# A two-layer diffusion trunk on one core: the final norm made on token rows, tile by tile, and each tile stored by itself

## The chip, the core and the metric

The kernel runs on one core of a Trainium2 chip. The number that counts is the device time of one execution in microseconds. The kernel before takes 3027.04 us, the median of 3 runs (3024.94 to 3028.75).

## What is computed

The reference is one inference step of a trunk of two layers over 128 prompt tokens and 512 latent tokens of width 1024. Each layer has a modulated RMS norm, three attention branches beside each other with gates and one output projection, a second norm, and a mixture of 16 experts of which each chooses its tokens. What follows the last layer is all that this case touches:

```
def rms_norm(x, g):
    xf = x.astype(jnp.float32)
    y = xf * lax.rsqrt(jnp.mean(xf * xf, axis=-1, keepdims=True) + EPS)
    return y.astype(x.dtype) * g
...
        x = x + gate2 * expert_choice_ffn(h, w_router, w1, w3, w2)   # end of a layer, for xp and for xs
...
    y_prompt = rms_norm(xp, final_norm)      # (1, 128, 1024)
    y_sample = rms_norm(xs, final_norm)      # (1, 512, 1024)
```

All data is fp32. The mean runs over the 1024 channels of a token, `final_norm` is one weight per channel.

## The kernel before

The residual `x` lies transposed: `x[:, k, t]` is a tile of 128 channels (partition) by 640 tokens (free), for k = 0 to 7; the 512 latent tokens are columns 0 to 511, the 128 prompt tokens are columns 512 to 639. In PSUM there are two tiles of 1024 columns (`mm[0]`, `mm[1]`), one of 1024 (`tp`) and two of 512 (`oo[0]`, `oo[1]`); each hands over by a counting semaphore pair (full, empty). The order on every engine is written out by hand; engines meet only at semaphores.

The experts run in 8 pairs. SyncE streams 24 weight chunks of 1 MB per pair through a ring of 6 buffers, ScalarE rounds each half chunk (`w_hi`), VectorE takes the rest (`w_lo`), TensorE multiplies. What a pair has made (`ye_hi`, `ye_lo`, one row per chosen token) is spread over the tokens by a matmul with a one-hot matrix `hot_t`.

The end of a layer, which the change touches, goes thus in the last layer:

- **Spread.** For k = 0 to 7 TensorE makes two matmuls of 512 columns into `oo[k % 2]` (L1612), and VectorE adds the result, times a gate, to `x[:, k, 0:512]` (`spread`, helper line L2164), which frees `oo[k % 2]` for k + 2. ScalarE squares each finished tile (`last_square`, L2137), VectorE adds the odd squares, GpSimd the even ones (L944).
- **Prompt.** The 16-row results of all experts for prompt tokens come back from DRAM (`ye_ptok`, L2134). TensorE makes the combination in 32 recorded matmuls into `tp` (`combine_p`, L1620), VectorE adds it in 8 instructions to the prompt columns, ScalarE squares those (L2139).
- **Sum of squares over channels.** It is a matmul with a matrix of ones (L1629, L1632), so that the sum of a token stands in every partition of its column.
- **rsqrt.** VectorE scales and adds EPS, ScalarE makes Ln and Exp (`first_rstd`, L1666 and L1668), and VectorE makes one Newton step (`refine_rstd`), all on 128 x 640 elements.
- **Scaling.** VectorE writes `h = x * final * rstd` in 8 instructions.
- **Turning.** For each of 5 token tiles TensorE transposes 8 blocks of `h` into `tp` (L1640), and ScalarE copies `tp` to `tok` (L1649), which holds token rows. There is one `tp`, so the tiles go one after another.
- **Stores.** When all five are done, SyncE issues the store of 4 latent tiles (2 MB, L825) and of the prompt tile (0.5 MB, L826).

Of the kernel before, what the change touches and what calls it, by code (L numbers as in the profile page):

```python
# [255 lines left out]

H_TILES, H_AT = [], {}
# [128 lines left out]
def build(nc, a):  # L388
    ctx = ExitStack()
    with ctx:  # L390
# [38 lines left out]
        tmp = [sb(f"tmp{i}", [P, T]) for i in range(3)]  # L429
        rstd = tmp_r = sb("rstd", [P, T])  # L430
        dw_tmp = [rounded(f"dw_tmp{i}", "tmp2", i * HALF * P, [P, HALF, P]) for i in range(2)]
        const = sb("const", [P, CONST_COLS])
# [111 lines left out]
        slot_in = [sem(f"slot{i}_in") for i in range(RING)]  # L544
        chunks_free = sem("chunks_free")
        mm_full = [sem(f"mm{i}_full") for i in range(2)]
        mm_empty = [sem(f"mm{i}_empty") for i in range(2)]
# [156 lines left out]
        def last_square(k):  # L704

            return (tmp[2][:, 0:NLAT], rstd[:, 0:NLAT], tmp[0][:, 0:NLAT], tmp[1][:, 0:NLAT],
                    *(flat[:, i * NLAT:(i + 1) * NLAT] for i in range(4)))[k]

        last_square_p = flat[:, 3 * D:4 * D].rearrange("p (k t) -> p k t", k=KT)

# [18 lines left out]
        def _(sp):  # L729
# [93 lines left out]

            sp.wait_ge(y_ready, 2)
            sp.dma_start(a["y_sample"][0].rearrange("(t p) c -> p t c", p=P), tok[:, 0:LT, :]).then_inc(y_sent, 16)  # L825
            sp.dma_start(a["y_prompt"][0], tok[:, PRT, :]).then_inc(y_sent, 16)  # L826
            sp.wait_ge(y_sent, 32)
            sp.wait_ge(new_sent, DEPTH * NEW_STORES * 16)
# [6 lines left out]
        def _(pool):  # L835
# [6 lines left out]
            for l in range(DEPTH):  # L842
# [98 lines left out]

                for k in (2, 4, 6):
                    pool.wait_ge(last_sq, l * (KT + 1) + k + 1)
                    last = pool.tensor_tensor(last_square(0), last_square(0), last_square(k), ALU.add)  # L944
                    pool.drain()
                pool.sem_inc(last_even, 1)

# [4 lines left out]
        def _(pe):  # L952
# [181 lines left out]
            for l in range(DEPTH):  # L1134
# [468 lines left out]
                if l + 1 < DEPTH:  # L1603
                    pe.wait_ge(small_in, SMALL_LOADS[l + 1] * 16)
                    wait_t_empty(pe, l, TR["cols_next"])
                    pe.transpose(tp[:, 0:NROWS], rows[:, :], ident[0:NROWS, 0:NROWS]).then_inc(t_full, 1)
                for k in range(KT):
                    j = OO["pairs"] + k
                    wait_o_empty(pe, l, j, PAIRS - 1)
                    for y, ready, n in ((ye_hi, ye_hi_ready, 2 * PAIRS * (l + 1)), (ye_lo, ye_done, PAIRS * (l + 1))):  # L1610
                        pe.wait_ge(ready, n)
                        last = pe.matmul(oo[j % 2][:, :], y[:, k * P:(k + 1) * P], hot_t[:, :],  # L1612
                                         start=(y is ye_hi), stop=(y is ye_lo))
                    last.then_inc(o_full[j % 2], 1)

                pe.wait_ge(ye_back, l * 16 + 16)
                wait_t_empty(pe, l, TR["combine_p"])
                for k in range(KT):
                    for g in range(2):
                        last = pe.matmul(tp[:, k * P:(k + 1) * P], ye_ptok[:, g, k * P:(k + 1) * P],  # L1620
                                         hotw_pt[:, g, :], start=(g == 0), stop=(g == 1))
                last.then_inc(t_full, 1)

                j = MM["norm1"]
# [9 lines left out]


            pe.wait_ge(h_ready, DEPTH * 2 * KT + 1)
            for t in range(TT):
                wait_t_empty(pe, DEPTH, t)
                for k in range(KT):
                    last = pe.transpose(tp[:, k * P:(k + 1) * P], h[:, k, t * P:(t + 1) * P], ident)  # L1640
                last.then_inc(t_full, 1)

# [4 lines left out]
        def _(act):  # L1647
# [98 lines left out]
            for l in range(DEPTH):  # L1746
# [384 lines left out]
                for k in range(KT):  # L2131
                    if k == 2:
                        act.wait_ge(ye_stored, 32 * PAIRS * l + (32 * PAIRS + 32))
                        act.dma_start(ye_ptok, a["ye_pr"].rearrange("e s c -> (e s) c")  # L2134
                                      .rearrange("(g p) c -> p g c", p=P)).then_inc(ye_back, 16)
                    wait_o_read(act, l, OO["pairs"] + k, PAIRS - 1)
                    act.activation(last_square(k), x[:, k, 0:NLAT], ACT.Square).then_inc(last_sq, 1)  # L2137
                wait_t_read(act, l, TR["combine_p"])
                act.activation(last_square_p, x[:, :, NLAT:T], ACT.Square).then_inc(last_sq, 1)  # L2139


            load_log()
            first_rstd(DEPTH, 0)
            for t in range(TT):
                wait_t_full(act, DEPTH, t)
                copy(tok[:, t, :], tp[:, :]).then_inc(t_empty, 1)
            act.drain()
            act.sem_inc(y_ready, 2)

# [4 lines left out]
        def _(dve):  # L2154
# [150 lines left out]
            dve.sem_inc(x_ready, 1)  # L2305
            dve.sem_inc(layer_free, 1)

            for l in range(DEPTH):
# [547 lines left out]
                for k in range(KT):  # L2856
                    spread(k, PAIRS - 1)
                    if k in (4, 6):
# [3 lines left out]
                dve.sem_inc(last_odd, 1)  # L2862
                wait_t_full(dve, l, TR["combine_p"])
# [7 lines left out]

            refine_rstd(DEPTH, 0, 0, D)
            for k in range(KT):
                last = stt(h[:, k, :], x[:, k, :], col("final", k), rstd[:, :], ALU.mult, ALU.mult)
            last.then_inc(h_ready, 1)

# [34 lines left out]
```

## Time and profile before

| | us |
|---|---|
| median of 3 runs | 3027.04 |
| the profiled execution, its own time | 3027.11 |
| its span in the profile | 3025.3 |
| TensorE busy in the span | 2827.1 (93%) |
| VectorE busy | 2013.2 (67%) |
| ScalarE busy | 1643.7 (54%) |
| last matmul of the last expert pair begins | 2966.43 |
| store of y_sample issued | 3017.04 |

The profiled execution is 1.8 us longer than its span: that much lies outside what the profile shows. Busy time is a sum over the whole span; the stretch of the change is the last 60 us, and in it no engine is busy for long. There the chain of waits must be read, not the shares. The granted clock of TensorE has two levels, 1.00 (2.4 GHz) and 0.50 (1.2 GHz); a slice with a number between holds a change from one to the other.

### The profile page before, as it was taken

The numbers are of one execution on the slowest core, as the hardware profiler recorded it, in microseconds if no ns is written. First come the engines' busy times: TensorE is split into PE (matmuls) and PEld (weight loads), VectorE is DVE, ScalarE is ACT, GpSimd is POOL, SyncE is SP. The second block draws the span as 40 slices with busy tenths as digits, with TensorE's granted clock in tenths as the row PEclk, the third lists the DMA queues.
The fourth block names the chain that finished last, engine by engine and source line by source line (L and its number), as shares of the span: only waits on it lengthen the run. The fifth ranks groups of instructions, "written<-read, shape, count | busy, mean of one in ns | idle before, by whom it ended". The sixth has DMA issues, their size and how long they took to land.

```text
span 3025.3 us, 45336 instructions
## 1 busy us (share of the span) xinstructions
PE 2827.1 (93%) x16026; PEld 2222.8 (73%) x16026; DVE 2013.2 (67%) x3103; ACT 1643.7 (54%) x2435; POOL 266.0 (9%) x294
## 2 busy tenths in 40 slices
PE   6999999989989999999989999999998999999995
PEld 3868966979947777777658797688896677777774
DVE  3463256473469999999845524655646799999994
ACT  3253344263257777777634524433524677777773
POOL 0050012030010000000002300200201000000000
PEclk9999999999989999999999999999999999999997
DMA  7102200222289999999821021013043799999991
GB/s 296 60 32 78 74 30 29 85 73 98 106 302 354 335 336 336 336 335 337 303 73 63 29 96 57 1 56 128 29 147 139 287 338 333 337 337 337 332 347 54
DMA packets 280123, 564.13 MB, mean 186 GB/s; under 512 B 14040, under 2 KB 19872, under 8 KB 279328
## 3 DMA queue, kind: packets, MB, share of 16 engines
q1 hardware_dynamic: 273056, 543.25, 50.2%
q10 hardware_dynamic: 4448, 9.87, 0.9%
q0 software_dynamic: 2464, 8.91, 0.8%
q8 instruction: 102, 1.67, 0.2%
q14 instruction: 53, 0.43, 0.0%
HBM read 546.36 MB, written 15.63 MB: 186 GB/s over the span
## 4 chain that ended last, share of the span: by engine, by line
PE 65%; DVE 14%; issue 7%; ACT 5%; ACTq 2%; POOL 2%; DVEq 1%; DMA 1%; POOLq 1%; SPq 0%
PE mm L1050 23%; PE mm L1571 20%; DVE w_lo L2156 7%; PE mm L1073 6%; PE mm L1103 2%; PE mm L1295 2%; DVE x L2164 2%; ACTq L2077 2%; POOL scratch L864 2%; ACT scratch L1649 1%; ACT w_hi L1649 1%; PE oo L1007 1%; DVE scratch L2156 1%; PE oo L1317 1%; POOLq L863 1%
## 5 line engine op out<-in xcount | busy, mean ns | idle before, releaser
L2156 DVE TENSOR_TENSOR w_lo<-ring,w_hi 128x1024 fp32r<-128x1024 f32 x768 | 911.9, 1219 | 86.6 <-ACT w_hi L1649 70.0
L1649 ACT ACTIVATE w_hi<-ring 128x1024 fp32r<-128x1024 f32 x768 | 803.4, 1059 | 277.9 <-PE mm L1571 255.4
L1050 PE MATMUL mm<-h_hi,ring_lo 128*128 128x320 f32 (+1 forms) x1344 | 315.1, 316 | 2.5 <-DVE h_lo L2156 2.0
L1050 PEld LDWEIGHTS mm<-h_hi,ring_lo 128*128 128x128 f32 (+1 forms) x1344 | 224.6, 189 | 16.3 <-issue 14.4
L1571 PE MATMUL mm<-w_lo,xa_hi 128*80 128x512 f32 x512 | 204.7, 400 | 18.1 <-DVE w_lo L2156 11.8
L2156 DVE TENSOR_TENSOR ring_lo<-ring,dw_hi 128x512 fp32r<-128x512 f32 (+1 forms) x104 | 70.1, 676 | 207.2 <-ACT dw_hi L1649 206.2
L1571 PE MATMUL mm<-w_lo,xb_hi 128*128 128x512 f32 x512 | 203.9, 398 | 0.0
L1571 PE MATMUL mm<-w_hi,xa_lo 128*80 128x512 f32 x512 | 202.6, 396 | 0.0
L1571 PE MATMUL mm<-w_hi,xa_hi 128*80 128x512 f32 x512 | 201.4, 393 | 0.0
L1571 PE MATMUL mm<-w_hi,xb_hi 128*128 128x512 f32 x512 | 200.0, 391 | 0.0
L1571 PE MATMUL mm<-w_hi,xb_lo 128*128 128x512 f32 x512 | 199.4, 389 | 0.0
L1649 ACT ACTIVATE dw_hi<-ring 128x512 fp32r<-128x512 f32 (+1 forms) x104 | 64.0, 619 | 226.2 <-PE mm L1050 225.3
L1649 ACT ACTIVATE scratch<-mm 16x1024 f32<-16x1024 f32 (+7 forms) x140 | 99.4, 720 | 103.4 <-PE mm L1103 42.0
L1050 PE MATMUL mm<-h_lo,dw_hi 128*128 128x320 f32 (+1 forms) x576 | 132.2, 311 | 0.0
L1050 PE MATMUL mm<-h_hi,dw_hi 128*128 128x320 f32 (+1 forms) x576 | 132.2, 311 | 0.0
L1571 PEld LDWEIGHTS mm<-w_lo,xa_hi 128*80 128x80 f32 x512 | 76.4, 149 | 61.4 <-DVE w_lo L2156 18.3
L923 POOL DMA_INDIRECT merged<-h_rows,stat x16 | 27.8, 1739 | 1041.5 <-DVE w_lo L2156 1001.0
L1050 PE MATMUL mm<-h_lo,dw_tmp 128*128 128x320 f32 x512 | 117.7, 311 | 0.0
L1050 PE MATMUL mm<-h_hi,dw_tmp 128*128 128x320 f32 x512 | 117.7, 311 | 0.0
L1743 ACT ACTIVATE scratch<-mm,stat 128x640 f32<-128x640 f32 (+1 forms) x80 | 56.6, 708 | 102.8 <-DVE stat L2292 102.8
L1571 PE MATMUL mm<-w_lo,hidb_hi 128*128 128x512 f32 x256 | 101.5, 397 | 11.7 <-DVE w_lo L2156 11.7
L1571 PEld LDWEIGHTS mm<-w_hi,xb_hi 128*128 128x128 f32 x512 | 96.1, 188 | 20.9
(325 smaller groups left out, 6071.7 us busy)
## 6 DMA issues: line engine op xcount, KB each, us to landing
ring<-in_w_ff SPq DMA_DIRECT2D x384, 1024.0 KB, 6.4
ring<-in_w_ada SPq DMA_DIRECT2D x48, 1024.0 KB, 7.4
ring<-in_w_gate SPq DMA_DIRECT2D x24, 1024.0 KB, 6.1
ring<-in_w_in SPq DMA_DIRECT2D x16, 1024.0 KB, 9.5
ring<-in_w_o SPq DMA_DIRECT2D x8, 1024.0 KB, 7.9
x_spill<-x SPq DMA_DIRECT2D x2, 2560.0 KB, 12.6
ring<-in_w_br_da SPq DMA_DIRECT2D x4, 1024.0 KB, 6.4
ring<-in_w_br_mla SPq DMA_DIRECT2D x4, 1024.0 KB, 5.2
```

The costliest lines, as they stand in the source:

```text
L863: pool.drain()
L864: pool.tensor_tensor(p1, p1, p2, ALU.add).then_inc(p_mixed, 1)
L1050: last = pe.matmul(out[0:width, lo:hi], w_, h_[:, k, lo:hi], start=(k == 0 and i == 0), stop=(k == KT - 1 and i == 2))
L1073: last = pe.matmul(h_out(j)[:, lo:hi], w_, o_[:, k, lo:hi], start=(k == 0 and i == 0), stop=(k == 3 and i == 2))
L1103: last = pe.matmul(mm[j % 2][:, 0:width], h[:, k, t * P:(t + 1) * P], weight(c, k, c0, c0 + width), start=(k == 0), stop=(k == KT - 1))
L1295: last = pe.matmul(mm[j % 2][:, at:at + hi - lo], ml_q[hd % 2][0:MQ, t * P:(t + 1) * P], ml_k[hd % 2][0:MQ, lo:hi], start=True, stop=True)
L1571: last = pe.matmul(out[0:rows_, bank:bank + 512], a_[:, k, 0:rows_], b_[n % SPLITS][:, kk, :], start=(k == 0 and i == 0), stop=(k == KT - ...
L1649: return act.activation(out, in_, ACT.Copy, scale=scale)
L1743: act.activation(out, mm[j % 2][:, 0:width], ACT.Exp, bias=stat[:, sum_at:sum_at + 1], accum_out=stat[:, sum_at + 16:sum_at + 17])
L2077: act.drain()
L2156: return dve.tensor_tensor(out, in0, in1, op)
L2164: return dve.scalar_tensor_tensor(out=out, in0=in0, scalar=s, in1=in1, op0=op0, op1=op1)
```

## The change

Nothing changes before the last spread of the last layer. From there:

- TensorE turns `x`, not `h`. While it spreads, it transposes block k - 2 of token tiles 0 and 1 into `mm[0]` and `mm[1]`, two transposes ahead of the matmuls of each k from 2 on, and blocks 6 and 7 behind the spread. Tile 2 goes into `oo[0]` and `oo[1]` behind `combine_p`, the prompt tile into `tp` when the prompt columns are done, and tile 3 into `mm[0]` when tile 0 has been read for the last time. The order of the output tiles is 0, 1, 2, prompt, 3.
- ScalarE squares each turned tile from PSUM in two halves of 512 columns with an accumulated sum per token (`accum_out`); Ln and Exp work on 2 columns for tiles 0 and 1, and on 3 columns for the others.
- VectorE adds the two halves, makes mean plus EPS, waits for Exp, makes the Newton step on 2 or 3 columns, and writes `tok = turned * rstd * final_row` straight from PSUM, two instructions of 512 columns per tile. The first mean stands in its order between the last spread and the prompt's additions.
- `final_row`, the weight as a row in all 128 partitions, is loaded by one broadcasting DMA (512 KB written), issued by SyncE behind the last weight chunk.
- SyncE stores each tile when it is ready.
- The squares of `x`, their additions on VectorE and GpSimd, the matmuls with ones, the scaling of `h`, the last transposes and ScalarE's copies are gone in the last layer.

```diff
+Y_ORDER = (0, 1, 2, PRT, LT - 1)
+        final_row = nc.alloc_sbuf_tensor_at("final_row", [P, D], FP32, offset=place["tmp2"])
+        def y_parts(n):
+            at = (mm[0], mm[1], None, tp, mm[0])[n]
+            return [oo[half][:, 0:512] if at is None else at[:, 512 * half:512 * half + 512] for half in range(2)]
...
 SyncE
-            sp.wait_ge(y_ready, 2)
-            sp.dma_start(a["y_sample"][0].rearrange("(t p) c -> p t c", p=P), tok[:, 0:LT, :]).then_inc(y_sent, 16)
-            sp.dma_start(a["y_prompt"][0], tok[:, PRT, :]).then_inc(y_sent, 16)
-            sp.wait_ge(y_sent, 32)
+            sp.wait_ge(lgt_ready, DEPTH)
+            sp.wait_ge(h_ready, DEPTH * 2 * KT)
+            sp.dma_start(final_row[:, :], a["final_norm"].partition_broadcast(P)).then_inc(final_in, 16)
+            for n, t in enumerate(Y_ORDER):
+                sp.wait_ge(y_ready, n + 1)
+                sp.dma_start(a["y_sample"][0][t * P:(t + 1) * P, :] if t < LT else a["y_prompt"][0], tok[:, t, :])\
+                    .then_inc(y_sent, 16)
+            sp.wait_ge(y_sent, 16 * TT)
...
 TensorE
+                def turn_y(out, t, k):
+                    return pe.transpose(out[:, k % 4 * P:(k % 4 + 1) * P] if out is oo[k // 4] else out[:, k * P:(k + 1) * P],
+                                        x[:, k, t * P:(t + 1) * P], ident)
                 for k in range(KT):
                     j = OO["pairs"] + k
                     wait_o_empty(pe, l, j, PAIRS - 1)
+                    if l + 1 == DEPTH and k >= 2:
+                        for t in range(2):
+                            if k == 2:
+                                wait_mm_empty(pe, DEPTH, t)
+                            turn_y(mm[t], t, k - 2)
...
+                if l + 1 == DEPTH:
+                    for k in (6, 7):
+                        wait_o_read(pe, l, OO["pairs"] + k, PAIRS - 1)
+                        for t in range(2):
+                            last = turn_y(mm[t], t, k)
+                            if k == 7:
+                                last.then_inc(y_turned, 1)
... (combine_p)
+                if l + 1 == DEPTH:
+                    for k in range(KT):
+                        last = turn_y(oo[k // 4], 2, k)
+                    last.then_inc(y_turned, 1)
+                    pe.wait_ge(x_ready, 1 + 2 * DEPTH)
+                    for k in range(KT):
+                        last = turn_y(tp, PRT, k)
+                    last.then_inc(y_turned, 1)
+                    pe.wait_ge(y_ready, 1)
+                    for k in range(KT):
+                        last = turn_y(mm[0], LT - 1, k)
+                    last.then_inc(y_turned, 1)
+                    break
...
 ScalarE
             load_log()
-            first_rstd(DEPTH, 0)
-            for t in range(TT):
-                wait_t_full(act, DEPTH, t)
-                copy(tok[:, t, :], tp[:, :]).then_inc(t_empty, 1)
-            act.drain()
-            act.sem_inc(y_ready, 2)
+            for lo, hi in ((0, 2), (2, TT)):
+                for n in range(lo, hi):
+                    act.wait_ge(y_turned, n + 1)
+                    for half, part in enumerate(y_parts(n)):
+                        act.activation(h_flat[:, 512 * (2 * n + half):512 * (2 * n + half + 1)], part, ACT.Square,
+                                       accum_out=stat[:, 2 * n + half:2 * n + half + 1])
+                act.drain()
+                act.sem_inc(y_squared, 1)
+                act.wait_ge(y_mean, 1 if lo == 0 else 2)
+                act.activation(stat[:, 32 + lo:32 + hi], stat[:, 24 + lo:24 + hi], ACT.Ln)
+                act.drain()
+                act.activation(stat[:, 32 + lo:32 + hi], stat[:, 32 + lo:32 + hi], ACT.Exp, scale=-0.5)\
+                    .then_inc(y_root, 1)
...
 VectorE
+            def y_mean_of(lo, hi):
+                dve.wait_ge(y_squared, 1 if lo == 0 else 2)
+                sums = stat[:, 2 * lo:2 * hi].rearrange("p (n h) -> p n h", h=2)
+                tt(stat[:, 24 + lo:24 + hi], sums[:, :, 0], sums[:, :, 1], ALU.add)
+                dve.drain()
+                ts(stat[:, 24 + lo:24 + hi], stat[:, 24 + lo:24 + hi], 1.0 / D, ALU.mult, EPS, ALU.add).then_inc(y_mean, 1)
... (behind spread(7), ahead of the wait for combine_p)
+                    y_mean_of(0, 2)
... (at the end)
+            dve.wait_ge(final_in, 16)
+            for lo, hi in ((0, 2), (2, TT)):
+                if lo:
+                    y_mean_of(lo, hi)
+                v, r_, t_ = stat[:, 24 + lo:24 + hi], stat[:, 32 + lo:32 + hi], stat[:, 40 + lo:40 + hi]
+                dve.wait_ge(y_root, 1 if lo == 0 else 2)
+                tt(t_, r_, r_, ALU.mult)
... (three more small operations, a drain behind each)
+                for n in range(lo, hi):
+                    for half, part in enumerate(y_parts(n)):
+                        at = slice(512 * half, 512 * half + 512)
+                        last = stt(tok[:, Y_ORDER[n], at], part, stat[:, 32 + n:33 + n], final_row[:, at],
+                                   ALU.mult, ALU.mult)
+                    dve.drain()
+                    dve.sem_inc(y_ready, 1)
```

## Rows read from the trace of the kernel before

**Rows 1.** Chain of waits, last 60 us: start us, duration us, engine, tile, line.
```profile
2970.72 3.30 PE oo L1612 x6
...
2977.51 5.17 PE tp L1620 x32
...
2984.93 1.06 ACT merged L2139
...
3001.62 1.98 PE tp L1640 x8
...
3003.63 1.03 ACT merged L1649
...
3015.95 1.02 ACT merged L1649
```

**Rows 2.** Stretches, TensorE: from:to, us, busy (count), granted clock, DMA share, GB/s.
```profile
2967.00:2968.00 1.00, 0.00 (x0) 1.00 0.00 0
...
2970.00:2971.00 1.00, 0.61 (x3) 0.74 0.15 29
...
2980.00:2981.00 1.00, 1.00 (x8) 0.64 0.00 0
2981.00:2982.00 1.00, 1.00 (x11) 1.00 0.00 0
...
2990.00:2992.00 2.00, 0.00 (x0) 0.74 0.00 0
```

**Rows 3.** Timeline of the spread, all engines: start, us, engine, line, operation, out<-in.
```profile
2971.74 0.63 PE L1612 MATMUL oo<-hot_t,ye_hi 128*128 128x512 f32 x1
2972.17 0.63 PE L1612 MATMUL oo<-hot_t,ye_lo 128*128 128x512 f32 x1
...
2974.72 0.68 DVE L2156 TENSOR_TENSOR rstd<-rstd,tmp 128x512 f32<-128x512 f32 x1
...
2977.70 0.75 DVE L2164 SCALAR_TENSOR_TENSOR x<-oo,mod,x 128x512 f32<-128x512 f32 x1
```

**Rows 4.** Timeline of TensorE: eight transposes at clock 1.00.
```profile
2877.45 1.04 PE L1524 MATMUL tp<-const,merged 128*128 128x128 f32 x8
```

**Rows 5.** Timeline of ScalarE: activations with accumulated sum, and table loads.
```profile
636.71 0.68 ACT L1964 ACTIVATE scratch<-mm,stat 128x512 f32<-128x512 f32 x1
...
637.37 0.29 ACT L1966 ACTIVATE stat<-stat,bc 128x1 f32<-128x1 f32 x1
...
229.60 1.28 ACT L1837 ACT_TABLE_LOAD   x1
231.70 0.22 ACT L1837 ACTIVATE scratch<-scratch 128x20 f32<-128x20 f32 x1 [0.82 <-DVE scratch L2161]
231.98 1.28 ACT L1839 ACT_TABLE_LOAD   x1
```

**Rows 6.** Timeline of VectorE: small operations, and larger ones on PSUM.
```profile
234.03 0.18 DVE L2161 TENSOR_SCALAR scratch<-scratch 128x20 f32<-128x20 f32 x1
234.28 0.18 DVE L2156 TENSOR_TENSOR scratch<-scratch 128x20 f32<-128x20 f32 x1
...
2969.91 1.41 DVE L2164 SCALAR_TENSOR_TENSOR x<-oo,mod,x 128x512 f32<-128x512 f32 x2 [0.63 <-PE oo L1612]
...
2982.70 2.16 DVE L2164 SCALAR_TENSOR_TENSOR x<-tp,mod,x 128x128 f32<-128x128 f32 x8 [4.25 <-PE tp L1620]
```

**Rows 7.** DMA issues, whole span: out<-in, queue, count, KB each, median us to landing.
```profile
h_rows<-merged ACTq DMA_DIRECT2D x8, 512.0 KB, 3.6
...
out_y_prompt<-merged SPq DMA_DIRECT2D x1, 512.0 KB, 7.4
...
ctx_in<-in_cache_mla_krope SPq DMA_DIRECT2D x2, 16.0 KB, 3.1
```

**Rows 8.** Timeline of SyncE's queue, last 122 us.
```profile
2903.43 42.79 SPq L819 DMA_DIRECT2D ring<-in_w_ff  x15
3017.04 0.39 SPq L825 DMA_DIRECT2D out_y_sample<-merged  x1
```

More of the change, by code:

```diff
@@ L545, in build @@
         chunks_free = sem("chunks_free")
+        y_turned, y_squared, y_mean, y_root, final_in = (sem("y_turned"), sem("y_squared"), sem("y_mean"), sem("y_root"),
+                                                         sem("final_in"))
         mm_full = [sem(f"mm{i}_full") for i in range(2)]
@@ L707, in last_square @@
                     *(flat[:, i * NLAT:(i + 1) * NLAT] for i in range(4)))[k]
+        def y_parts(n):
+            at = (mm[0], mm[1], None, tp, mm[0])[n]
+            return [oo[half][:, 0:512] if at is None else at[:, 512 * half:512 * half + 512] for half in range(2)]
+        h_flat = h[:, :, :].rearrange("p k t -> p (k t)")
         last_square_p = flat[:, 3 * D:4 * D].rearrange("p (k t) -> p k t", k=KT)
@@ L940, in _ @@
                 pair(PAIRS - 1, True)
-                for k in (2, 4, 6):
+                for k in (2, 4, 6) if l + 1 < DEPTH else ():
                     pool.wait_ge(last_sq, l * (KT + 1) + k + 1)
@@ L945, in _ @@
                     pool.drain()
-                pool.sem_inc(last_even, 1)
+                if l + 1 < DEPTH:
+                    pool.sem_inc(last_even, 1)
         @block.tensor
@@ L1633, in _ @@
                 last.then_inc(mm_full[j % 2], 1)
-            pe.wait_ge(h_ready, DEPTH * 2 * KT + 1)
-            for t in range(TT):
[L1638 to L1641, printed above, removed]
         @block.scalar
@@ L2135, in _ @@
                                       .rearrange("(g p) c -> p g c", p=P)).then_inc(ye_back, 16)
[L2136 to L2139, printed above, removed]
-            load_log()
-            first_rstd(DEPTH, 0)
-            for t in range(TT):
-                wait_t_full(act, DEPTH, t)
-                copy(tok[:, t, :], tp[:, :]).then_inc(t_empty, 1)
-            act.drain()
-            act.sem_inc(y_ready, 2)
+                    if l + 1 < DEPTH:
+                        wait_o_read(act, l, OO["pairs"] + k, PAIRS - 1)
+                        act.activation(last_square(k), x[:, k, 0:NLAT], ACT.Square).then_inc(last_sq, 1)
+                if l + 1 < DEPTH:
+                    wait_t_read(act, l, TR["combine_p"])
+                    act.activation(last_square_p, x[:, :, NLAT:T], ACT.Square).then_inc(last_sq, 1)
+            load_log()
+            for lo, hi in ((0, 2), (2, TT)):
[11 more added lines that the diff above has]
+                    .then_inc(y_root, 1)
         @block.vector
@@ L2857, in _ @@
                     spread(k, PAIRS - 1)
-                    if k in (4, 6):
+                    if k in (4, 6) and l + 1 < DEPTH:
                         dve.wait_ge(last_sq, l * (KT + 1) + k)
@@ L2861, in _ @@
                         dve.drain()
-                dve.sem_inc(last_odd, 1)
+                if l + 1 < DEPTH:
+                    dve.sem_inc(last_odd, 1)
+                else:
+                    y_mean_of(0, 2)
                 wait_t_full(dve, l, TR["combine_p"])
@@ L2869, in _ @@
                     dve.sem_inc(s, 1)
[L2872 to L2875, printed above, removed]
+            dve.wait_ge(final_in, 16)
[6 more added lines that the diff above has]
+                dve.drain()
+                tt(t_, t_, v, ALU.mult)
+                dve.drain()
+                ts(t_, t_, -0.5, ALU.mult, 1.5, ALU.add)
+                dve.drain()
+                tt(r_, r_, t_, ALU.mult)
+                dve.drain()
+                for n in range(lo, hi):
[3 more added lines that the diff above has]
+                                   ALU.mult, ALU.mult)
+                    dve.drain()
+                    dve.sem_inc(y_ready, 1)
         return nc
```

## The prediction

> **What bounds the kernel now.** I read the page first: TensorE is busy 93% of the span, and the chain that ended last lies on it for 65%. None of that bears on this change, which touches only the last 60 us. There I read the chain of waits in order of time. The reader is to see in it that behind the spread (2970.72 to about 2978) one engine works at a time: 32 matmuls for the prompt from 2977.51, which end at 2982.68, one square on ScalarE at 2984.93, and then nothing that the rows show of transposes until 3001.62 [rows 1]. Between lie the ones-matmuls, Ln and Exp, the Newton step and the scaling, one behind the other on 640 columns. From 3001.62 each tile takes eight transposes (1.98) and one copy (1.03), and as there is one PSUM tile for them, these alternate: (3015.95 - 3003.63) / 4 = 3.08 us per tile [rows 1]. Only then, at 3017.04, is a store issued [rows 8]; the span ends at 3025.3, 8.3 us later, with every engine idle. From the end of the prompt's matmuls to the last copy (3016.97) that is 34.3 us, and 42.6 us to the end of the span.
>
> **The spread gets longer.** Two matmuls of a k start 0.43 us apart (2971.74, 2972.17) while the clock is low, which it is from 2970.7 on [rows 2, 3]. Eight transposes take 1.98 at the low clock [rows 1] and 1.04 at the high one [rows 4], so 0.25 and 0.13 each. Before, TensorE is not full in this stretch: per k its work is 0.86, and the chain through VectorE (0.75 for the addition, [rows 3]) gives about 1.04. With two transposes per k the work is 0.86 + 0.50 = 1.36, and TensorE becomes the bound of the spread. Six k's (2 to 7) from 2970.72 make 8.2, to 2978.9; with 0.2 until the last result stands and 0.04 + 0.75 on VectorE the last addition ends at 2979.9, against 2978.45 before: 1.4 later. (The two VectorE additions of squares, 0.68 each [rows 3], go away; they delayed k = 5 and k = 7 by some 0.6, and that gain is in this count, because TensorE is the bound now.) At the high clock the transposes would be hidden and the spread end at 2978 or before: that is the other end, 1.9 better. I take the low clock, since the fall within 2970 to 2971 follows a pause of TensorE around the last expert results (idle from 2967 to 2968 [rows 2]), and that pause stays. The transposes of blocks 6 and 7: two fit in before the last addition ends, two come behind it, 0.5, so that the prompt's matmuls begin at 2980.4 and not at 2977.5.
>
> **The prompt's matmuls** take 5.17 before, of which about 3.3 at the low clock, until it rises at 2980.6, and 1.9 at the high one [rows 1, 2]. I take the same 5.2 and hold C = 2985.6 as their end: 2.9 later than before. If the clock did not rise at all they would take 32 x 0.22 = 7.0.
>
> **Beside them, hidden.** ScalarE squares tiles 0 and 1. The next instruction behind an activation with accumulated sum on 128 x 512 starts 0.66 after it (636.71 to 637.37 [rows 5]), so a half costs 0.66, a tile 1.32, two tiles 2.6: from 2980.4 to 2983.1. VectorE's mean, two small operations of 0.25 each with their drain [rows 6], gives 2983.7; Ln 0.22, a table load 1.28, Exp 0.22 give 2985.5. VectorE waits for these squares in front of the prompt's additions; behind it in its order stand these additions and then the whole output, and their input comes at C = 2985.6, so that wait has 1.9 us of cover and the root 2.3 more. If the squares took 2 us longer, the excess would move everything. The table set with Ln is loaded early, in the idle time of the spread. The squares of x, GpSimd's additions (hidden before too) go away for nothing gained.
>
> **The weight row.** SyncE's last weight chunk is issued at 2946.2 [rows 8]; the broadcast goes out behind it and is wanted at C + 2.2 = 2987.8. No row shows a broadcast of this size. The nearest, 512 KB between SBUF and DRAM, land in 3.6 and 7.4 [rows 7]; priced by the byte from the 16 KB load (3.1, [rows 7]) it would be 99 us. I take under 10, by the rows of its size, and cost it at nothing: 41.6 us cover it.
>
> **Behind C, the path.** (1) Eight additions for the prompt, 2.16 [rows 6], to 2987.8; in this time TensorE turns tile 2 and ScalarE squares it, done by 2988.1 at the high clock, 2989 at the low one. (2) Four small operations of the Newton step at 0.25 with drain: 1.0, to 2988.8. (3) Tile 0: two instructions of 128 x 512 on PSUM with two operands, 0.70 each when back to back [rows 6], with a drain 1.5, to 2990.3. The prompt tile is turned in parallel and squared by 2991.2 at the latest. (4) Tile 3 needs the buffer of tile 0: eight transposes, 1.04 at the high clock and 1.98 at the low one. Before, the clock falls at about 2990.5, some 2.4 us after the last matmul [rows 2]; here only transposes with pauses follow C. I take the low clock, to 2992.3. (5) Its squares 1.32 and a drain, to 2993.75. (6) Now the root for tiles 2, prompt and 3. ScalarE's load for Ln is issued ahead of the wait of its activation: at L1837 the load ran at 229.60 and the activation waited for VectorE behind it [rows 5]. So the load (1.28) covers VectorE's mean (0.5). Ln 0.22, load 1.28, Exp 0.22 follow: 3.1 in all, to 2996.85. (7) Newton step 1.0, to 2997.85. (8) Three tiles at 1.5, to 3002.35. Tiles 0 and 1 leave VectorE before 2992, so their stores are long gone. Sum behind C: 16.75, against 34.3 before.
>
> **The stores.** The last one is 512 KB of the same shape as h_rows from the same buffer, 3.6 from issue to landing [rows 7]. Two others go out 1.5 and 3.0 us before it. The upper bound is the 7.4 of y_prompt, which stood behind 2 MB; the lower one is 3.1, the landing of 16 KB [rows 7]. I take 3.6 and 0.4 for the end behind the landing (3017.48 + 7.4 = 3024.9 against 3025.3): 4.0 against 8.3 before.
>
> ScalarE's table loads are where the Trainium skill gives another answer. The trace has a load at Ln and another at the Exp behind it, 1.28 each [rows 5]. The Trainium skill (ScalarE: Activation LUTs, "Table sets: the hidden batching unit") says that one set holds both functions and that a change from one to the other needs no load; the trace disagrees here. By the page the sum would be two loads less, 2.6.
>
> The Trainium skill speaks against the split stores: DMA: Bandwidth & Descriptors, "Bandwidth", asks for 1 MiB or more per DMA for 75% of the peak. The row of the 512 KB store is the duration that is used here; that its rate falls when three follow each other no row shows.
>
> **Sum.** 2.9 lost up to C; 34.3 - 16.75 = 17.55 won behind it; 4.3 won at the stores: 18.95. Span 3025.3 - 18.95 = 3006.35. The profiled execution is 3027.11, 1.8 above its span, and 0.07 from the median of 3027.04, so the time is 3008.2.
>
> **Rivals.** (a) *The clock stays at 1.2 GHz through the prompt's matmuls*, because they begin behind a spread with short pauses and stop-and-go work. For it: the clock was low for 10 us of nearly full TensorE before [rows 2]. Against: it rose 3.1 us after the dense stretch began. C moves by 1.85: 3010.1. Chance 0.15.
> (b) *The last three stores get in each other's way*: at 7.4 for the last landing, 3.8 more: 3012.0. For it: the row of y_prompt. Against: its 2 MB in front, for which here are at most 1 MB, sent earlier. Chance 0.08.
> (c) *Ln and Exp need no load between them*: 3005.6. Against: rows 5 show one at either. Chance 0.03.
> (d) *The transposes and squares cost less than counted* (the clock high for tile 3, or the spread at its upper end): 0.9 to 2.8 less, 3005.4 to 3007.3. Chance 0.10.
> (e) *Slower than before: the weight row comes late.* All 128 partitions read the same 4 KB of DRAM, and VectorE waits for it in front of all ten output instructions. Every microsecond above 41.6 is paid in full; from 41.6 + 18.85 = 60.4 the kernel is no faster, from 66.5 it is slower by over 0.2%. At 99 us the time is 3008.2 + 57.4 = 3065.6. For it: no row shows such a load. Against: both rows of its size. Chance 0.03.
> (f) *The waits in VectorE's order eat the gain*: if tiles 0 and 1's squares held it 4 us past C (each half at 2 us instead of 0.66), 3012. Chance 0.03.
>
> **From these to the numbers.** The forecast has 0.58, with its own range 3006.5 to 3010. The predicted time is 3008.2. The range 3003.5 to 3013 leaves out (e), the far ends of (b) and (c) together with (d), and what I have not thought of. About 0.2% (6 us) is what a measurement of this kernel can tell from no change. Faster by over 0.2% needs less than 3021: all cases but (e), 0.96; within 0.2%: 0.01; slower: 0.03.
>
> **What would show it right or wrong.** In the changed profile: the last addition of the spread at about 2979.9, C at 2985.6 and a clock that is 1.00 before C; a table load on ScalarE ahead of the wait at Ln and one at each Exp; the root for tiles 0 and 1 ready ahead of the prompt's last addition; a wait of VectorE for ScalarE from about 2991.8 to 2996.85 as the only long one behind C; three pairs of output instructions at the end, and 4 us behind them. The prediction is wrong in its core if VectorE waits for the weight row, if the prompt's matmuls begin later than 2981, or if the last store takes over 5 us.

## The result, and the profile after

The changed kernel takes 2998.64 us (median of 4 runs, 2996.76 to 3001.06), the kernel before in the same measurement 3025.99 (4 runs). The ratio is 0.9911, with a 95% interval of 0.9894 to 0.9928: faster by 0.9%, or 27.3 us. I had forecast 3008.2 and 19 us of gain; the time lies below my range. In a later series, with 5 runs of the changed kernel and 15 of the one before, the ratio came out as 0.9925 (0.9912 to 0.9939): 2999.68 against 3023.09, a gain of 23.4 us.

The profiled execution of the changed kernel took 2997.64 us at a span of 2995.8. The chain of waits of its last 36 us (start, duration, engine, tile, line) answers to [rows 1]:

```profile
2961.68 1.12 ACT ye_hi L1690
...
2971.90 0.76 DVE x L2214
...
2973.14 3.59 PE tp L1654 x32
2976.76 0.35 DVE x L2214
...
2981.76 1.11 PE mm L1626 x8
2982.89 0.60 ACT h L2190
...
2984.24 1.28 ACT L2195
...
2985.79 1.28 ACT L2197
...
2988.29 0.75 DVE merged L2214
...
2992.11 0.66 DVEq L2951
```

L1690 is the activation of the last expert result, L1654 is the prompt's combination, L1626 the transposes, L2190 the squares, L2195 Ln and L2197 Exp, L2214 VectorE's additions and outputs. The activation of the last expert result (2961.68 here, 2966.85 before) is where what lies ahead of the change ends. I call what comes before its start the head and what follows the tail, and count from there: the tail takes 34.1 us here, 58.5 before. The two heads differ by 5.2 us, though the only thing that the change adds to them is the issue of the weight row, which nothing in them waits for.

The clock, from the stretches of TensorE (from:to, us, busy, granted clock, DMA share, GB/s), against [rows 2]:

```profile
2966.00:2967.00 1.00, 1.00 (x5) 0.50 0.19 16
...
2968.00:2969.00 1.00, 1.00 (x5) 0.67 1.03 418
2969.00:2970.00 1.00, 1.00 (x6) 1.00 0.99 410
...
2985.00:2986.00 1.00, 0.00 (x0) 0.87 0.36 143
```

It was low for 3.4 us in the spread, not for 10.2, and it was high from there to the last transpose (it fell at 2985.7, and the last eight transposes ran from 2981.76 to 2982.87). The timeline of TensorE (start, us, line, operation) shows one k at either clock:

```profile
2966.87 0.63 PE L1626 MATMUL mm<-const,x 128*128 128x128 f32 x2
2967.15 0.78 PE L1639 MATMUL oo<-hot_t,ye_hi 128*128 128x512 f32 x1
2967.72 0.63 PE L1639 MATMUL oo<-hot_t,ye_lo 128*128 128x512 f32 x1
2968.15 0.63 PE L1626 MATMUL mm<-const,x 128*128 128x128 f32 x2
...
2970.10 0.44 PE L1626 MATMUL mm<-const,x 128*128 128x128 f32 x2
2970.29 0.48 PE L1639 MATMUL oo<-hot_t,ye_hi 128*128 128x512 f32 x1
2970.61 0.40 PE L1639 MATMUL oo<-hot_t,ye_lo 128*128 128x512 f32 x1
2970.95 0.44 PE L1626 MATMUL mm<-const,x 128*128 128x128 f32 x2
```

At the low clock a k takes 2968.15 - 2966.87 = 1.28 us (forecast 1.36), at the high one 2970.95 - 2970.10 = 0.85. ScalarE and VectorE behind it:

```profile
2973.07 0.60 ACT L2190 ACTIVATE h<-mm 128x512 f32<-128x512 f32 x1 [5.31 <-PE mm L1626]
2973.56 0.19 ACT L2190 ACTIVATION_READ_ACCUMULATOR h<-mm 128x1 f32 x1
2973.66 0.59 ACT L2190 ACTIVATE h<-mm 128x512 f32<-128x512 f32 x1
...
2977.54 0.20 ACT L2197 ACTIVATE stat<-stat 128x2 f32<-128x2 f32 x1
...
2984.24 1.28 ACT L2195 ACT_TABLE_LOAD   x1
2985.53 0.21 ACT L2195 ACTIVATE stat<-stat 128x3 f32<-128x3 f32 x1
2985.79 1.28 ACT L2197 ACT_TABLE_LOAD   x1
2987.08 0.21 ACT L2197 ACTIVATE stat<-stat 128x3 f32<-128x3 f32 x1
```

```profile
2976.76 2.16 DVE L2214 SCALAR_TENSOR_TENSOR x<-tp,mod,x 128x128 f32<-128x128 f32 x8 [0.80 <-PE tp L1654]
2979.30 0.40 DVE L2206 TENSOR_TENSOR stat<-stat 128x2 f32<-128x2 f32 x2 [0.38 <-issue]
...
2984.46 0.17 DVE L2211 TENSOR_SCALAR stat<-stat 128x3 f32<-128x3 f32 x1
2987.32 0.41 DVE L2206 TENSOR_TENSOR stat<-stat 128x3 f32<-128x3 f32 x2 [2.70 <-ACT stat L2197]
...
2991.36 1.41 DVE L2214 SCALAR_TENSOR_TENSOR merged<-mm,stat,final_row 128x512 f32<-128x512 f32 x2
```

A half tile is squared in 0.59 (2973.07 to 2973.66; I had 0.66 from [rows 5]). The load for Ln begins right behind the last squares, before VectorE's mean is there, and VectorE then waits 2.70 for the root. The DMA issues (out<-in, queue, count, KB each, median us to landing), against [rows 7]:

```profile
out_y_sample<-merged SPq DMA_DIRECT2D x4, 512.0 KB, 2.6
...
final_row<-in_final_norm SPq DMA_DIRECT2D x1, 512.0 KB, 5.9
out_y_prompt<-merged SPq DMA_DIRECT2D x1, 512.0 KB, 2.6
```

The last store is issued at 2992.83, 3.0 us ahead of the end of the span (8.3 before, [rows 8]). The weight row was issued at 2941.3, landed 5.9 us later, and was wanted at 2979: VectorE never waited for it.

### The profile page after: what moved, and what is told of

The parts are those of the page before. It is cut to its first block, busy times and chain, and to the rows that moved or that the text cites. A ratio compares the mean times of both kernels' runs of the same rounds, so it can differ in the third digit from the quotient of the medians.

```text
span 2995.8 us, 45311 instructions
## 1 busy us (share of the span) xinstructions
PE 2807.7 (94%) x16004; PEld 2209.9 (74%) x16004; DVE 2010.7 (67%) x3110; ACT 1640.6 (55%) x2445; POOL 262.3 (9%) x291
## 4 chain that ended last, share of the span: by engine, by line
PE 65%; DVE 14%; issue 7%; ACT 5%; ACTq 2%; POOL 2%; DMA 2%; DVEq 1%; POOLq 1%; SPq 0%
PE mm L1067 24%; PE mm L1588 20%; DVE w_lo L2206 7%; PE mm L1090 6%; PE mm L1312 2%; DVE x L2214 2%; PE mm L1120 2%; ACTq L2118 2%; POOL scratch L880 2%; ACT scratch L1690 1%; ACT w_hi L1690 1%; DVE scratch L2206 1%; PE oo L1334 1%; PE oo L1024 1%; POOLq L879 1%
## 5 line engine op out<-in xcount | busy, mean ns | idle before, releaser
L1690 ACT ACTIVATE w_hi<-ring 128x1024 fp32r<-128x1024 f32 x768 | 803.5, 1059 | 277.6 <-PE mm L1588 255.1
L1067 PEld LDWEIGHTS mm<-h_hi,ring_lo 128*128 128x128 f32 (+1 forms) x1344 | 225.0, 189 | 16.3 <-issue 14.4
L1690 ACT ACTIVATE dw_hi<-ring 128x512 fp32r<-128x512 f32 (+1 forms) x104 | 64.1, 619 | 227.7 <-PE mm L1067 225.2
L1690 ACT ACTIVATE scratch<-mm 16x1024 f32<-16x1024 f32 (+7 forms) x140 | 99.4, 720 | 101.1 <-PE mm L1120 40.1
```

Source lines behind the costliest of these rows:

```text
L1067: last = pe.matmul(out[0:width, lo:hi], w_, h_[:, k, lo:hi], start=(k == 0 and i == 0), stop=(k == KT - 1 and i == 2))
L1690: return act.activation(out, in_, ACT.Copy, scale=scale)
```

## The experiments

Tails are given in us from the start of the activation of the last expert result to the end of the span; C is the end of the prompt's matmuls, from the same point; "low" is the length of the low-clock stretch that begins some 3.6 us behind this point. For the kernel before, the first profile has tail 58.5, C 15.8, low 10.2; for the changed one 34.1, 15.0, 3.4. The expectations call rival accounts by letters: A and B are on the head, T and L on the clock in the spread, S is on the stores, R on the root.

**The changed kernel again** (no edit).

> The changed kernel as it is, run again beside the kernel before. From the last expert result's activation to the end of the span it took 34.1 us, against 58.5 before; the first profiles lie 29.5 apart, and 5.2 of that comes from ahead of the change, where TensorE stood at the low clock for 116 us in one run and 133 in the other. Theory A (what lies ahead of the change is the same, and differs only by where the low-clock stretches fall in a run): the tail measures 34 to 35 again, the stretch ahead moves by several us from run to run with the low-clock time, and the ratio stays at 0.991 to 0.993. Theory B (the changed program is faster ahead of the change too): the stretch ahead is 5 us shorter than before again. In the tail: low clock for 3.4 us in the spread if the transposes raise it (theory T), anything from 3.4 to 10 if it is luck of the moment (theory L).

Measured: 0.9925 (0.9912 to 0.9939), 2999.68 us. Tail 34.6, C 15.05, low 3.4. The head ended at 2962.6. The tail is some 0.4 longer than in the first profile because here the clock fell while tile 3 was turned: its eight transposes took 1.53, not 1.09.

**The kernel before again** (no edit), and once more later.

> The kernel before as it is, submitted as a kernel of its own, for a second profile of it. Theory A: ratio 1.000 within its interval, and the time from the start of the span to the last expert result's activation (2966.9 us in the first profile) anywhere in 2960 to 2970, with the low-clock time. Theory B: 2966 to 2968 again. The low-clock stretch in the last spread: 10 us again if only matmuls with pauses are there (theory T), 3.4 to 10 by luck (theory L).

> The kernel before, a third profile, for the same question: theory T expects the low stretch in the spread to be over 3.4 us or absent in most of the profiles without transposes; theory L expects 3.4 here as in those with them. The start of the last expert result's activation within 2960 to 2967, as in all profiles so far.

Measured: 0.9998 (0.9989 to 1.0007) for the second (3020.78, 11 runs), 3025.21 for the single run of the third. The second profile has its head end at 2962.4, tail 56.0, C 13.3, and no low stretch in the spread at all; the third 2965.0, 58.4, 15.8 and 10.2. From the timelines of TensorE, the prompt's matmuls in the second and then in the third:

```profile
2971.83 3.84 PE L1620 MATMUL tp<-scratch 128*128 128x128 f32 x32
```

```profile
2975.45 5.33 PE L1620 MATMUL tp<-scratch 128*128 128x128 f32 x32
```

The same program takes 3.84 or 5.33 for the same 32 matmuls, by the clock that it meets. And the head, whose work no kernel here changes, ended anywhere from 2960.5 to 2967.0 in the sixteen profiles of this case. It goes largely with the time that TensorE spent at the low clock in it: the four profiles with the least (116.1 to 119.5 us) have heads of 2960.5 to 2961.7, the five with the most (133.1 to 136.5) of 2963.9 to 2967.0. Theory A holds and B falls: in the second profiles the head of the kernel before ended at 2962.4 and that of the changed one at 2962.6. The first profile of before had one of the slowest heads, and its series (medians of 3026 to 3027, of 3 and 4 runs) lay some 3 us above the later ones (3023.1 and 3023.6, of 15 and 23 runs).

**Tiles 0 and 1 turned behind the spread**, twice.

```diff
... (in the loop of the spread)
-                    if l + 1 == DEPTH and k >= 2:
-                        for t in range(2):
...
-                            turn_y(mm[t], t, k - 2)
... (behind it)
-                    for k in (6, 7):
-                        wait_o_read(pe, l, OO["pairs"] + k, PAIRS - 1)
...
+                    for k in range(KT):
+                        if k >= 6:
+                            wait_o_read(pe, l, OO["pairs"] + k, PAIRS - 1)
                         for t in range(2):
                             last = turn_y(mm[t], t, k)
```

> The changed kernel, but tiles 0 and 1 are transposed behind the spread instead of inside it: 16 transposes moved. Theory T (the transposes inside the spread keep TensorE full, and so the clock comes back 3.4 us after its fall instead of 10 us): the low stretch is 10 us again, the spread ends no earlier than before (11.6 us after the last expert result), and the prompt's matmuls, which begin behind the 16 transposes, are half at the low clock: the tail takes 34.1 + 3 to 5. Theory L (luck): low stretch of any length, and the tail is longer only by the 12 transposes that move behind the spread, at 0.13 each 1.6, less what the spread gains from being without them (0.5): 35.2.

> The changed kernel with its transposes behind the spread, a second profile. Theory T: a low stretch of 6.8 us again or longer, C at 15.6 or later. Theory L: 3.4 us, and then C at 15.0 or before and a tail of 34 to 35.

Measured: 0.9925 (0.9912 to 0.9939), 3001.69 against 2999.68 in the same series, with the same ratio; the second was a single run of 2996.14. First profile: low 6.8, C 15.6, tail 35.6. Second: low 3.4, C 14.7, tail 33.8. So at 3.4 of low clock the transposes inside the spread are worth nothing: C is 0.3 earlier without them. The times do not tell the two kernels apart, and of theory T's 3 to 5 us at most 1.4 appeared, in the first profile, 0.5 of it ahead of C.

**Stores as before.**

```diff
+            sp.wait_ge(y_ready, TT)
+            sp.dma_start(a["y_sample"][0].rearrange("(t p) c -> p t c", p=P), tok[:, 0:LT, :]).then_inc(y_sent, 16)
+            sp.dma_start(a["y_prompt"][0], tok[:, PRT, :]).then_inc(y_sent, 16)
```

> The changed kernel with the stores of before: one wait for all five tiles, then 2 MB and 0.5 MB. Theory S (splitting the stores is worth what the profile shows: 3.0 us from the last issue to the end of the span, against 8.3 from the first issue before): 5.3 us slower than the changed kernel. Rival (the split stores get in each other's way or cost issue time on SyncE): under 3 us.

Measured: 3004.72, 5.0 above the changed kernel in the same series; 0.9941 (0.9928 to 0.9955). Tail 39.4, 4.8 and 5.3 longer than the two of the changed kernel; the 5.3 is against the one with the same clock to the end of the transposes. Its issues:

```profile
out_y_sample<-merged SPq DMA_DIRECT2D x1, 2048.0 KB, 6.6
out_y_prompt<-merged SPq DMA_DIRECT2D x1, 512.0 KB, 7.4
```

Theory S holds.

**The transposes alone, on the kernel before**, then each three times.

```diff
                     wait_o_empty(pe, l, j, PAIRS - 1)
+                    if l + 1 == DEPTH and k >= 2:
+                        for t in range(2):
...
+                            pe.transpose(mm[t][:, (k - 2) * P:(k - 1) * P], x[:, k - 2, t * P:(t + 1) * P], ident)
```

> The kernel before with one part of the change alone: the twelve transposes of x inside the last spread, into mm[0] and mm[1], which nobody reads. All else is as before. In two profiles of the kernel before the low-clock stretch in the spread was 10.2 us long in one and absent in the other; in three of the changed kernel it was 3.4 each time. Theory T (the transposes fill TensorE's pauses and bring the clock back early): low for 3.4 us here too, and the prompt's matmuls end 15 us after the last expert result. Theory L (it is luck, and the transposes only add their time): any length from 0 to 10, the spread longer than before at an equal clock by up to 1.0. In both the time of the kernel is within 2 us of before, since the rest of the tail is unchanged.

> The kernel before with each of the twelve transposes in the spread made three times (36, six ahead of each k from 2 on; nobody reads them). Theory T (transposes in the spread bring the clock back): the low stretch is 3.4 us. At the high clock a transpose costs 0.13, so six cost 0.8 per k and TensorE binds the spread at 0.46 + 0.8 = 1.25 per k: the prompt's matmuls end 16.5 us after the last expert result. Theory L: any length; with 10 us of low clock six transposes cost 1.5 per k, 2.35 in all, and the end is at 23.

Measured: 0.9994 (0.9985 to 1.0002) for the single ones; low 3.4, C 14.4, tail 57.1. With three times as many: low 3.4, C 16.1, tail 58.8 (one run, 3027.3). Theory T had forecast both low stretches and, for the first, C of 15; theory L allowed both. The TensorE timeline of the second shows what six transposes cost at the high clock:

```profile
2975.49 0.82 PE L1615 MATMUL mm<-const,x 128*128 128x128 f32 x6
2976.07 0.48 PE L1618 MATMUL oo<-hot_t,ye_hi 128*128 128x512 f32 x1
2976.38 0.40 PE L1618 MATMUL oo<-hot_t,ye_lo 128*128 128x512 f32 x1
2976.61 0.82 PE L1615 MATMUL mm<-const,x 128*128 128x128 f32 x6
```

A k takes 1.12 there (2975.49 to 2976.61), with no pause of TensorE in the rows, against 1.25 expected.

**The tile stores alone, on the kernel before.**

```diff
                 copy(tok[:, t, :], tp[:, :]).then_inc(t_empty, 1)
-            act.drain()
-            act.sem_inc(y_ready, 2)
+                act.drain()
+                act.sem_inc(y_ready, 1)        # and SyncE stores tile t at y_ready t + 1
```

> The kernel before with another part alone: each token tile is stored when it has been copied (y_ready counts tiles), nothing else. The last copy ends as before, and then only 512 KB have to land. Theory S (the store of the last tile alone takes 3.0 us from issue to the end of the span, as in the changed kernel, because the others have landed): 5.3 us faster than before. Rival: with 3.1 us between tiles the stores are already apart, so the gain can be no larger than this; smaller, under 3, if the landing of a small store is bound by something else here.

Measured: 0.9982 (0.9973 to 0.9990), 5.5 us faster than before (3018.02 against 3023.55). Tail 51.1, low 3.4, C 13.7. Behind C it takes 37.4, where all six profiles with the stores of before and the rest of its tail take 42.7, whatever the clock had done up to C: 5.3 less, the size that theory S had. This one part of the change is worth a quarter of it.

**No logarithm for the last three tiles** (it leaves out a step of the root, so their scale is wrong).

```diff
-                act.activation(stat[:, 32 + lo:32 + hi], stat[:, 24 + lo:24 + hi], ACT.Ln)
+                act.activation(stat[:, 32 + lo:32 + hi], stat[:, 24 + lo:24 + hi], ACT.Ln if lo == 0 else ACT.Copy)
```

> The changed kernel with the logarithm left out for the last three tiles (a copy in its place, so y is wrong in their scale): no table has to be changed for them. Theory R (the two table loads behind the last squares stand on the path, 1.28 each): 2.5 us faster than the changed kernel, and the tail of 34.4 becomes 31.9; VectorE's wait between its mean and the Newton step falls from 2.7 to about 0.5. Rival (the first of the two loads is hidden behind VectorE's mean, which takes 0.5): 2.1.

Measured: tail 32.0, low 3.4, C 15.05. That is 2.1 shorter than the first profile of the changed kernel, which had the same clock for tile 3, and 2.6 shorter than the second. The wait of VectorE for the root, which was 2.70:

```profile
2990.48 0.41 DVE L2206 TENSOR_TENSOR stat<-stat 128x3 f32<-128x3 f32 x2 [0.55 <-ACT stat L2197]
```

2.15 less, as the rival had it in which VectorE's mean hides part of the first load. The run time (3000.1, ratio 0.9919, 0.9903 to 0.9935) can't tell it from the changed kernel, because heads vary by more; its head ended at 2967.0.

**One table, a root for each tile.** Sqrt and a reciprocal in place of Ln, Exp and the Newton step; order 0, 1, 2, 3, prompt.

```diff
... (ScalarE, for each tile n)
+                act.wait_ge(y_mean, n + 1)
+                act.activation(stat[:, 32 + n:33 + n], stat[:, 24 + n:25 + n], ACT.Sqrt).then_inc(y_root, 1)
... (VectorE)
+            def y_root_of(n):
+                dve.wait_ge(y_root, n + 1)
+                dve.reciprocal(stat[:, 40 + n:41 + n], stat[:, 32 + n:33 + n])
```

> A version meant to be faster than the changed kernel, with the complete output: the root is made with Sqrt on ScalarE and a reciprocal on VectorE, so that only one table is needed and no Newton step; each tile has its own root as soon as it is squared; tile 0 is written ahead of the prompt's additions, tile 3 is turned into its buffer at once, and the prompt tile goes last. Theory R (the tail behind the prompt's matmuls is bound by the batch of three tiles waiting for one root with its loads): from the end of the prompt's matmuls VectorE has 2.2 of additions, and per tile 1.5 of output and 0.6 of small operations for four tiles, 10.6 in all, against 16.1 in the changed kernel: 5.5 us faster. Rival (handing over between ScalarE and VectorE four times more eats it): under 3 us faster.

Measured: 2995.06, ratio 0.9905 (0.9888 to 0.9923); tail 28.9, low 3.4, C 15.04. In the tail that is 5.2 to 5.7 less than the changed kernel, as theory R had it, and in the median 4.6, against the changed kernel in an earlier series. The edit does several things at once: no table change, no Newton step, a root for each tile, and tile 0 written ahead of the prompt's additions. The run without the logarithm puts 2.1 on the table changes; how the other 3.1 divide was not measured.

**The root wholly on ScalarE, the last tile stored in halves.**

```diff
+                    act.activation(h_flat[:, 1024 * n:1024 * (n + 1)], (mm[0], mm[1], None, mm[0], tp)[n][:, :], ACT.Square,
+                                   accum_out=stat[:, 2 * n:2 * n + 1])
...
+                act.activation(stat[:, 32 + n:33 + n], stat[:, 2 * n:2 * n + 1], ACT.Sqrt, bias=bias, scale=1.0 / D)\
```

> A step further from the version with one table: ScalarE squares a tile in one instruction of 1024 columns (tile 2, which lies in two PSUM tiles, in two) and makes Sqrt of sum / 1024 + EPS itself, so VectorE has only the reciprocal and the two output instructions per tile; the last tile is stored in two halves. If VectorE is what binds behind the prompt's matmuls (1.4 of output and 0.65 of small operations per tile, four tiles), 0.4 per tile is saved and up to 0.7 at the last store: 2 us faster than that version, tail 27. If the wait for ScalarE binds instead, under 1.

Measured: 2993.21, ratio 0.9899 (0.9883 to 0.9916); tail 27.2, 1.7 below the version before it, where 2 was expected. It has the shortest tail and the lowest median, and by its ratio it is 30 us faster than the kernel before; from the version before it the interval of the ratio does not tell it apart. VectorE's last stretch in it has no wait left:

```profile
2987.43 0.16 DVE L2369 RECIPROCAL stat<-stat 128x1 f32<-128x1 f32 x1
2987.67 1.41 DVE L2223 SCALAR_TENSOR_TENSOR merged<-mm,stat,final_row 128x512 f32<-128x512 f32 x2
2989.20 0.16 DVE L2369 RECIPROCAL stat<-stat 128x1 f32<-128x1 f32 x1
2989.44 1.62 DVE L2223 SCALAR_TENSOR_TENSOR merged<-tp,stat,final_row 128x512 f32<-128x512 f32 x2
```

**One transpose per k in the changed kernel, and the kernel before without VectorE's additions of squares in the spread** (the second leaves out channels of the sum, so its y is wrong in scale).

> The changed kernel with half of the transposes inside the spread: one per k (tile 0), tile 1 behind it. Low for 3.4 us was seen in all six profiles with two per k; without any it was 10.2, 0, 3.4 and 6.8. Theory T (they fill the pauses): 3.4, or 6.8 if half the dose does not do. Theory L: any. The tail is the changed kernel's, 34.1 to 34.6, plus up to 0.8 for six transposes that move behind.

> The kernel before without VectorE's two additions of odd squares in the last spread (the sum of squares then lacks channels, so y is wrong in scale); VectorE's wait for those squares stands behind the spread. They delayed k = 5 and k = 7: at an equal clock the spread ends 0.5 to 0.7 earlier. It is also one more look at a spread without transposes. Low stretch with transposes inside: 3.4 us in nine profiles of nine; without: 10.2, 0, 3.4, 6.8. Theory T: not 3.4, or 3.4 seldom; theory L: 3.4 mostly.

Measured, one run each: with one per k low 3.4, C 14.4, tail 33.5 (3000.4), so C and the tail are 0.6 shorter than with two per k. Without the additions low 3.4, C 13.2, tail 55.9 (3020.07): C is 0.5 earlier than in the version with tile stores, which had the additions at the same clock (13.7).

**The clock, over all.** Low stretch in the spread with transposes inside: 3.4 us in nine profiles of nine. Without: 10.2, none, 10.2 (the kernel before), 6.8, 3.4 (turned behind), 3.4 (tile stores), 3.4 (no additions). Theory T's strict form, that without transposes the clock stays low for longer or does not fall at all, fell with the three looks of 3.4. The version with tile stores has the spread of the kernel before, instruction for instruction. The stretches of TensorE from the fall of the clock on, in the kernel before, in that version and in the changed kernel (columns as above):

```profile
2970.47:2973.88 3.41, 3.16 (x7) 0.50 0.41 88
```

```profile
2964.24:2967.65 3.41, 3.24 (x7) 0.50 0.41 98
```

```profile
2965.26:2968.67 3.41, 3.14 (x11) 0.50 0.46 137
```

TensorE is busy for 3.1 to 3.2 of the 3.4 us in all three. Behind them the clock stayed low in the first, for 6.8 us more, and rose in the other two. The starts of the matmuls in the first two stretches agree to 0.02 us, counted from the last expert result; both have the gap that the transposes fill in the third (2972.17 to 2972.79 in the first, 0.62 where 0.43 is enough). So the same work in the same place is followed by either clock, and what TensorE did in this stretch does not decide it alone. Against luck as the whole answer stand the nine of nine with transposes inside. That they bring the clock back is likely and not shown; what else decides it stays open.

## Why the prediction was wrong

By its own steps, from the profiled executions:

| step | forecast | measured |
|---|---|---|
| head ends (taken as before) | 2966.85 | 2961.68 |
| end of the spread, behind that | 13.05 | 10.97 |
| C, behind that | 18.75 | 15.04 |
| C to the end of the last output | 16.75 | 16.05 |
| last store and end | 4.0 | 3.0 |
| sum, with 1.8 outside the span | 3008.2 | 2997.6 |

The difference of 10.6 is 5.2 + 3.7 + 0.7 + 1.0. The 3.7 up to C is 2.1 in the spread and 1.6 in the prompt's matmuls.

**The first 5.2** is a term that I put at nothing without a reason: how far the head moves from run to run. I took a single profile's head as the kernel's. It was at the slow end of a spread of 6.5 us, and my range had no term for that. Against the gain of 23.4 us from more runs, the forecast 18.95 was short by 4.5.

**The step that failed** is the clock in the spread: "I take the low clock, since the fall within 2970 to 2971 follows a pause of TensorE around the last expert results ..., and that pause stays". The fall stayed (3.5 to 3.8 us behind the last expert result in all but one profile). What I did not ask is when the clock comes back. I had the rise of [rows 2], 10.2 us later, as if it belonged to the place; it came after 3.4. I then took "the same 5.2" for the prompt's matmuls, about 3.3 of it at the low clock, but wholly at the high clock they take 3.6. So C, which I had put 2.9 later than before, was 0.8 earlier. At an equal clock (low for 3.4) it is 13.7 without the change and 15.0 with it: the change costs 1.3 at this place, 0.7 for the transposes in the spread (14.4 in the kernel before with them) and the remaining 0.6 for blocks 6 and 7 and the pause ahead of them. Why the clock came back after 3.4 us stays open; that it did is in all nine profiles with transposes inside.

**The rivals.** Rival (d), cost of transposes and squares lower, pointed the right way with a chance of 0.10 and a floor of 3005.4; it had the spread at a high clock but not the prompt's matmuls, and the time lies below its floor by more than the head's 5.2. Rival (a) had the sign of the clock wrong. (e), the weight row late, did not happen: 5.9 us. (b), stores in each other's way, did not: 2.6 us each.

**Right:** the order of what ends last behind C; the table loads (two on the path; the load at Ln begins ahead of its wait and covers the mean, the wait left is 2.70 and falls to 0.55 without loads); the Newton step (0.97 from 2987.32 to 2988.29); 1.53 per output tile; tiles 0 and 1 wholly hidden (their root was ready at 2977.74, the additions ended at 2978.92, so 1.2 us to spare where I had 2.3, since C came earlier); and the way of the stores' gain, of which I had the size as 4.3 where it was 5.0 to 5.5. The 0.7 behind C is 0.9 for the clock of tile 3, which was high in this profile against my guess (1.11 for its transposes, not 1.98), and 0.1 for cheaper squares, less 0.3 that I had not counted: VectorE issues for 0.38 between the last addition and its first small operation. My step (6) gave 3.1 for terms that add up to 3.0; it measured 3.08. In the second profile the clock fell among these transposes, so that part of the 0.9 is luck.

On ScalarE's tables the profile after agrees with the one before: both the Ln and the Exp of the last three tiles have their load, of 1.28 each (2984.24 and 2985.79), and without the logarithm both loads are gone. The Trainium skill (ScalarE: Activation LUTs, "Table sets: the hidden batching unit") has both functions in one set, with a single load for the two; the trace disagrees. On small stores, the Trainium skill (DMA: Bandwidth & Descriptors, "Bandwidth") asks for 1 MiB or more per DMA for 75% of the peak. That is about the rate, which no run here tests by itself. What counts at the end of this kernel is when the last bytes land: 512 KB landed in 2.6 us against 6.6 for 2 MB and 7.4 for the 512 KB behind them, and splitting won 5 us, because three of the five parts had landed, and the fourth was on its way, when VectorE was done (2992.77).

## What to carry to other kernels

At the end of a kernel count what stands behind the last result, and store every part as soon as it is there: this part alone gave 5.3 to 5.5 us of 23. A sum of squares accumulated per token leaves 2 or 3 columns for the small operations where the transposed form worked on 640, but then the table changes and a batch of tiles behind one root are what binds; here a root for each tile from one table was worth 5.2 us more. And take two or more profiles of the kernel before before building on a stretch of low clock or on an absolute time: the head, the same work in all kernels here, differed by 6.5 us, and the tail of the kernel before by 2.5 us.

## What the runs showed of the hardware that I had not expected

- The clock of TensorE in one and the same stretch of one program was low for 10.2 us, for 10.2 us, and not at all in three executions, and C moved by 2.5 us with it; in another kernel with the same spread it was low for 3.4.
- A DMA of 512 KB that reads one 4 KB row for all 128 partitions landed in 5.9 us (6.3 in the second profile). Others of its size took 2.6 (the stores by tile), 3.6 (h_rows) and 7.4 (the prompt's store behind 2 MB), so it is within their range, and nothing near the 99 us that a price by the byte would give.
- Six transposes ahead of a 512-column matmul take 0.58 at the high clock from their first start to the start of that matmul (2975.49 to 2976.07, in the kernel with three times as many), 0.10 each. The 0.13 each of [rows 4] is counted to the end of the last one, so the two are not the same measure.
